# A search for the sample's best 256 keys: from 32 partitions to 128, with TensorE adding the parts

## The reference

```python
def _dsa_attend(q, qi, wi, kv, kidx, q_pos):
    n_sel = min(DSA_TOPK_MAX, lk // 4)
    ...
        idx_s = jnp.einsum('bthd,bsd->bths', qib, kidx) * (IDX_DIM ** -0.5)
        score = jnp.einsum('bth,bths->bts', wib * (IDX_HEADS ** -0.5), jax.nn.relu(idx_s))
        score = jnp.where(causal[None], score.astype(jnp.float32), NEG)
        top_s, top_i = lax.top_k(score, n_sel)
        ok = top_s > 0.5 * NEG
        kvs = kv[b_ix, top_i]
        ...
        p = _masked_softmax(s, ok[:, :, None, None, :])
        o = jnp.einsum('btghn,btngd->btghd', p.astype(kvs.dtype), kvs[:, :, :, 1])
```

## Time and profile before

| | us |
|---|---|
| median of 3 runs | 2259.28 |
| lowest and highest of them | 2257.66, 2259.74 |
| the profiled execution's own time | 2261.38 |
| its span in the profile | 2259.6 |
| PE busy, share of the span | 1815.2, 80% |
| DVE busy | 1120.3, 50% |
| ACT busy | 497.0, 22% |
| POOL busy | 264.0, 12% |

### The profile page before, as it was taken

The page is one execution under the profiler, slowest core; times in us unless marked ns, Lnnn a source line. Parts: engine busy times, 40 slices in busy tenths (PEclk is TensorE's granted clock), DMA queues, the critical chain, the costliest instruction groups (busy, mean ns, idle before and its releaser), DMA issues. The chain is left out here.

```text
span 2259.6 us, 27405 instructions
## 1 busy us (share of the span) xinstructions
PE 1815.2 (80%) x10205; PEld 1046.9 (46%) x10205; DVE 1120.3 (50%) x2591; ACT 497.0 (22%) x1087; POOL 264.0 (12%) x358
## 2 busy tenths in 40 slices
PE   7589999976999988967999878777866775377776
PEld 2367666633445434426666545454533332134332
DVE  0211682275777631223136999726646898021223
ACT  0300001054655400021111000024424331010111
POOL 0011020001544200000010000011122220000000
PEclk9799999987999987988999999888978897598888
DMA  6431351042000076601111101000020000999851
GB/s 250 172 132 61 109 204 63 1 155 76 1 1 1 1 249 162 171 22 63 38 61 36 39 20 39 20 0 1 1 75 1 1 1 7 266 212 227 218 160 36
DMA packets 85872, 189.31 MB, mean 84 GB/s; under 512 B 11531, under 2 KB 48493, under 8 KB 77226
## 3 DMA queue, kind: packets, MB, share of 16 engines
q1 hardware_dynamic: 57996, 120.13, 17.6%
q0 software_dynamic: 10464, 46.45, 5.9%
q10 hardware_dynamic: 17280, 20.98, 3.9%
HBM read 172.57 MB, written 19.12 MB: 85 GB/s over the span
## 5 line engine op out<-in xcount | busy, mean ns | idle before, releaser
L714 PE MATMUL banks<-hT,w_in 128*128 128x352 f32 x1632 | 492.1, 463 | 39.8 <-DVE qdT L782 18.8
L714 PEld LDWEIGHTS banks<-hT,w_in 128*128 128x128 f32 x1632 | 309.8, 191 | 219.3 <-DVE qdT L782 21.1
L2212 PE MATMUL banks<-w_out,mix 128*128 128x512 f32 (+1 forms) x576 | 269.9, 627 | 4.9 <-DVEq L2722 2.5
L710 PE MATMUL banks<-w_in,hT 128*128 128x264 f32 (+5 forms) x1008 | 221.9, 376 | 15.3 <-DMA w_in<-in_w_in 15.3
L710 PEld LDWEIGHTS banks<-w_in,hT 128*128 128x128 f32 (+1 forms) x1008 | 174.3, 188 | 51.5 <-DMA w_in<-in_w_in 15.6
L2212 PEld LDWEIGHTS banks<-w_out,mix 128*128 128x128 f32 (+1 forms) x576 | 107.4, 190 | 153.1 <-issue 146.4
L2228 DVE TENSOR_TENSOR y<-banks,gate_rows 128x512 f32<-128x512 f32 x32 | 22.1, 691 | 232.7 <-PE banks L2212 232.7
L1297 POOL TENSOR_SCALAR nsa_p<-nsa_p,nsa_sum,gates 128x640 f32<-128x640 f32 (+7 forms) x128 | 100.5, 796 | 226.2 <-DVE nsa_sum L1242 226.2
L824 ACT ACTIVATE mix<-banks 128x352 f32<-128x352 f32 x48 | 21.9, 464 | 412.4 <-PE banks L714 382.7
L1134 ACT ACTIVATE nsa_p<-nsa_p,nsa_negmax 128x640 f32<-128x640 f32 (+7 forms) x128 | 92.6, 725 | 29.0 <-DVE nsa_negmax L1123 28.5
L1123 DVE CUSTOM_DVE_ANT_0 nsa_p<-banks,wide_masks 128x640 f32<-128x640 f32 (+7 forms) x128 | 84.0, 703 | 22.7 <-PE banks L1109 22.7
(11 more groups left out here) (492 smaller groups left out, 2431.9 us busy)
## 6 DMA issues: line engine op xcount, KB each, us to landing
w_in<-in_w_in SPq DMA_DIRECT2D x24, 1056.0 KB, 5.0
ada_w<-in_ada SPq DMA_DIRECT2D x24, 1024.0 KB, 4.8
ds_ring<-in_diff_pairs SPq DMA_DIRECT2D x88, 256.0 KB, 5.5
ns_ring<-in_sel_pairs SPq DMA_DIRECT2D x88, 128.0 KB, 2.9
ds_ring<-in_dsa_pairs SPq DMA_DIRECT2D x88, 128.0 KB, 3.1
ds_ring<-in_diff_pairs ACTq DMA_DIRECT2D x40, 256.0 KB, 7.2
w_out<-in_l_w_out SPq DMA_DIRECT2D x4, 2048.0 KB, 20.6
ns_ring<-in_sel_pairs ACTq DMA_DIRECT2D x40, 128.0 KB, 4.2
```

The lines of the kernel that those rows point to most:

```text
L710: last = pe.matmul(bank[0:rows, 0:n], k.hT[:, a, r0:r0 + rows], w[:, j % slots, a, 0:n], start=(a == 0), stop=(a == KT - 1))
L714: last = pe.matmul(bank[:, 0:cn], w[:, j % slots, a, m * P:(m + 1) * P], k.hT[:, a, c0:c0 + cn], start=(a == 0), stop=(a == KT - 1))
L2212: last = pe.matmul(k.bank[u % 2][0:n, :], k.mix[:, a, r0:r0 + n], self.w[:, a, h * 512:(h + 1) * 512], start=a == 0, stop=a == KT - 1)
```

## The change

The class `SampleSearch` replaces `top_mask` for the sample. Each query's scores are laid on four partitions of 512 (the 32 scores of the new keys lie beside the fourth part; the other three have a very small number there), so one count covers 128 partitions x 544. Its sum, `search_seen`, is one column of 128 partial counts. PE multiplies it with a 128x128 matrix that has a 1 where two partitions belong to the same query, and every partition then finds the query's total in bank 7 (`total`). VectorE waits for it (`totalled`) and goes on with three small operations in place of four. The scan and the last passes stay as they were, on 32 partitions.

```diff
-def attend_pairs(k, name, units, base, blocks=None, between=None):
+def attend_pairs(k, name, units, base, blocks=None, between=None, search=None):
...
-        out_bank = lambda u: k.bank[6 + units[u]["tile"] % 2]
+        out_banks = 2 if search is None else 1
+        out_bank = lambda u: k.bank[6 + units[u]["tile"] % out_banks]
...
-                    if begin and i >= 2:
-                        pe.wait_ge(A.finished, i - 1)
+                    if begin and i >= out_banks:
+                        pe.wait_ge(A.finished, i - out_banks + 1)
...
                     turn(u, x)
+                    if search:
+                        search.add_parts(pe)
                     if behind:
                         values(*behind)
...
+                if search:
+                    for _ in range(3):
+                        next(between)
...
-                    while ended and e - ended[0][0] >= 2:
+                    while ended and e - ended[0][0] >= 2 and not search:
                         finish(ended.pop(0)[1])
...
                     copy(u, x)
+                    while ended and search:
+                        finish(ended.pop(0)[1])
...
+class SampleSearch:
...
+    def add_parts(self, pe):
+
+        if self.n < self.counts:
+            self.n += 1
+            pe.wait_ge(self.counted, self.n)
+            pe.matmul(self.total, self.same[:, :], self.seen[:, :], start=True, stop=True).then_inc(self.totalled, 1)
+
+    def count(self, dve, v, threshold, op):
+        dve.tensor_scalar(self.ge, v, threshold, None, op, ALU.add, accum_out=self.seen[:, :]).then_inc(self.counted, 1)
+
+    def steps(self, dve):
...
+        self.count(dve, v[:, :], 0.0, ALU.is_ge)
+        yield
+        dve.wait_ge(self.totalled, 1)
+        link(dve.tensor_scalar(found[:, :], self.total, float(TOPK), -1.0, ALU.is_lt, ALU.mult))
+        for n, bit in enumerate(range(30, -1, -1)):
+            link(dve.tensor_scalar(tried[:, :], found[:, :], 1 << bit, None, ALU.bitwise_xor))
+            self.count(dve, upper[:, :] if bit >= 16 else v[:, :], tried[:, :].bitcast(F32), ALU.is_ge)
+            yield
+            dve.wait_ge(self.totalled, n + 2)
+            link(dve.tensor_scalar(step[:, :], self.total, float(TOPK), float(1 << bit), ALU.is_ge, ALU.mult))
+            link(dve.tensor_tensor(found[:, :], found[:, :], step[:, :], ALU.bitwise_xor))
```

More of the change, by code:

```diff
@@ L1727, in dsa_prompt @@
             sample_index(k, ws)
-            choice = top_mask(k, k.nc.vector, ws, "sample_top", [(k.sample_score[:, :], k.sample_sel[:, :])], TOPK, NS,
-                              scratch=k.qiT[0:NS, :, :].rearrange("p a n -> p (a n)"))
-            attend_pairs(k, "dsa", units, 4, None, chain(keep_dsa_sample(k, k.nc.vector), choice))
+            search = SampleSearch(k, ws, k.qiT[0:NS, :, :].rearrange("p a n -> p (a n)"))
+            attend_pairs(k, "dsa", units, 4, None, chain(keep_dsa_sample(k, k.nc.vector), search.steps(k.nc.vector)), search)
@@ new lines, with __init__ @@
+class SampleSearch:
+    PART = PAST // 4
+    def __init__(self, k, st, scratch):
+        self.k, self.scratch = k, scratch
+        self.v = k.sb(st, "search_scores", [P, self.PART + NS])
+        self.upper = k.sb(st, "search_upper", [P, self.PART + NS], BF16)
+        self.upto = k.sb(st, "search_upto", [P, PAST + NS])
+        self.ge = self.upto[:, :].bitcast(BF16)[:, 0:self.PART + NS]
+        self.found, self.tried, self.step = (k.sb(st, f"search_{x}", [P, 1], I32) for x in ("found", "tried", "step"))
+        self.seen = k.sb(st, "search_seen", [P, 1])
+        self.of_query = k.sb(st, "search_of_query", [P, NS])
+        self.same = k.sb(st, "search_same_query", [P, P])
+        self.need = k.sb(st, "search_need", [NS, 1])
+        self.counted = k.sem(st, "search_counted")
+        self.totalled = k.sem(st, "search_totalled")
+        self.total = k.bank[7][:, 0:1]
+        self.counts, self.n = 33, 0
+    def add_parts(self, pe):
[6 more added lines that the diff above has]
+    def steps(self, dve):
+        k, v, upper, found, tried, step = self.k, self.v, self.upper, self.found, self.tried, self.step
+        link = lambda ins: k.dve_order.link(dve, ins)
+        score, m = k.sample_score, k.sample_sel
+        link(dve.tensor_reduce(self.of_query[:, :], k.const("ident").rearrange("p (x n) -> p n x", n=NS), X, ALU.add))
+        dve.tensor_copy(self.same[:, :].rearrange("p (x n) -> p x n", n=NS), self.of_query[:, :].unsqueeze(1).to_broadcast([P, P // NS, NS]))
+        dve.memset(v[0:3 * NS, self.PART:], TAKEN)
+        for j in range(4):
+            last = dve.tensor_copy(v[NS * j:NS * (j + 1), 0:self.PART], score[:, self.PART * j:self.PART * (j + 1)])
+        link(dve.tensor_copy(v[3 * NS:, self.PART:], score[:, PAST:PAST + NS]))
+        link(dve.tensor_copy(upper[:, :], v[:, :].bitcast(BF16)[:, 1:2 * (self.PART + NS):2]))
+        self.count(dve, v[:, :], 0.0, ALU.is_ge)
[9 more added lines that the diff above has]
+            link(dve.tensor_tensor(found[:, :], found[:, :], step[:, :], ALU.bitwise_xor))
+        kth = found[:, :].bitcast(F32)
+        self.count(dve, v[:, :], kth, ALU.is_gt)
+        yield
+        dve.wait_ge(self.totalled, self.counts)
+        kth, equal = kth[0:NS], self.scratch[:, 0:PAST + NS]
+        link(dve.tensor_scalar(self.need[:, :], self.total[0:NS], -1.0, float(TOPK), ALU.mult, ALU.add))
+        link(dve.tensor_scalar(equal, score[:, :], kth, None, ALU.is_equal))
+        yield
+        link(dve.tensor_tensor_scan(self.upto[0:NS, :], k.const("ones", NS)[:, 0:1].to_broadcast([NS, PAST + NS]), equal, 0.0, ALU.mult, ALU.add))
+        yield
+        link(dve.scalar_tensor_tensor(equal, self.upto[0:NS, :], self.need[:, :], equal, ALU.is_gt, ALU.mult))
+        link(dve.scalar_tensor_tensor(m[:, :], score[:, :], kth, equal, ALU.is_lt, ALU.add))
+        link(dve.tensor_scalar(m[:, :], m[:, :], NEG, None, ALU.mult))
```

## The result

The changed kernel takes 2204.3 us (median of 4 runs, 2199.88 to 2206.78) against 2259.51 us before (median of 4 runs, 2257.66 to 2272.97), or 55.2 us less. The ratio on record is 0.9729, 95% interval 0.9707 to 0.9752; the two medians themselves divide to 0.9756. The forecast was 2209 us.

The account below looks back on a forecast made before the run. The prediction took VectorE, mostly its search counts, to bound the stage. The loop's 142.0 us plus 7 of allowances and a 4.8 us later start made 153.8 against 203.8, 50 us less: 2209 us, range 2196 to 2228.

Parts of the forecast that it names:

- Counts and small operations: In the search loop, shorter counts and three small operations a step in place of four take 55 us off VectorE.
- The later start: At the stage's opening, copied queries and search setup, 6.3 us together, delay the first maxima by about 4.8 us.
- An add: On PE, each of 33 products that total the counts costs 0.3 us, with bounds of 0.14 and 0.54.
- PE becomes the bound: In steps without scores, PE runs through at 2.35 us a step and VectorE's 2.05 are hidden.
- lockstep rival: Counts end after PE reaches the add, 3.5 us a step; if in half of 36 steps, 2229 us; 18%.
- One bank (part 4): One output bank replaces two: a tile's first products wait for the previous multiplication out; PE loses 1.2 us in the last tile.
- The loop: First transposes to last multiplication: 15.4 us for tiles 0 and 1, 97.7 for 2 to 6, 28.9 for 7; 142.0.
- allowances: In the loop, 4 us for partly half clock and 3 us for the way between engines, making 149.
- half-clock rival: PE keeps the half clock in this stage and the kernel is 34 us slower, 2293 us; 4%.
- The sum: For the stage, 149 us, or 153.8 with the delayed opening, against 203.8: 50 us less.

Follow-up runs that it names:

- short counts: Kernel before with every count over 544 of 2080 columns on its 32 partitions, no adds or new layout: stage 156.99 us, median 2207.59 us.
- early start: Changed kernel with query copies and same-query matrix made in the stage ahead, search setup behind the first maxima: stage 145.42 us, median 2204.19 us.

## Why the prediction was right

The time was right, and the mechanism in its main part: VectorE bounded the stage by its counts, the counts were cut to a third, and the stage got shorter by what VectorE lost. Step by step:

- **Counts and small operations, 55 us off VectorE.** Right: 0.78 us a count, and of the 61.8 us that VectorE's work in the loop fell by, 5.9 only moved ahead of the loop, which leaves 55.9. The short counts alone take 54.6 us off the stage. The Trainium skill (VectorE: DVE Perf Modes, "The perf-mode tier table") would have a bf16 count at about half the time of an fp32 one; the groups show 779 ns for both, so the trace disagrees again.
- **The later start, 4.8 us.** Measured 4.9, but not by its terms: 6.3 us of work less a wait of 1.75 make 4.55. The work took 5.9 us (1706.21 to 1712.15), and only 1.06 of the wait could hide it, since VectorE still idles 0.69 us ahead of the work. That the start lay on the path, the early start shows by giving 4.4 of it back.
- **An add, 0.3 us.** Too much. It is 0.31 us from an add to the products only where PE has waited; where PE runs through it is 0.21, and the step grows by 0.11 to 0.12 (2.15 against 2.03 or 2.04), a little under the lower bound of 0.14. The second add of a doubled pair costs 0.22.
- **"PE becomes the bound" with VectorE's 2.05 us hidden.** The step that failed, though it did not cost the forecast. It holds in about half of the steps, those in which PE runs through, 2.15 us without scores in place of the 2.35 laid out; in most of the others PE waits for VectorE, which is not hidden there, and over the loop either one's microsecond counts for 0.6. The lockstep rival fails by its own sign: PE waits 4.9 us for counts, under the 10 that it named, and VectorE never for a total.
- **One bank (part 4).** It was priced as a loss of 1.2 us in the last tile; PE waits 1.04 there. But the earlier place of the multiplication, which comes with it, is worth 7.3 us in the kernel before, 5.7 with short counts and 7.9 in the changed one. The prediction laid the changed lists out with that place and so had it in its 142.0; it did not see it as a gain, and the 15.0 us of VectorE's waits before, on a line of their own, 12.8 of them such waits, were not read.
- **The loop, 142.0 laid out and 149 with allowances.** Measured 137.0: 14.4 for tiles 0 and 1 (15.4), 94.3 for tiles 2 to 6 (97.7), 28.4 for tile 7 (28.9). The layout was 5 us long, 3.4 of them in tiles 2 to 6: PE's work was 85.1 us there, with the shorter adds in it, where 87.3 were laid out, and it idled 9.2 against 10.4. The 7 us of allowances were not needed: the granted clock was 0.84 only in the first 14.4 us, behind a stretch in which PE had worked 4.1 of 12.8 us, then 1.00 for 94.3 with PE busy 85.1, and 0.95 at the end, so the half-clock rival was far off. The Trainium skill (TensorE: Matmul & The Clock Gate, Part 1) says that activity lifts the clock; the trace agrees.
- **The sum.** The stage shrank by 61.8 us where 50 were forecast, but the two profiles' spans differ by 54.7 only: the profile that the sum was made against had a next stage near the short end of its spread, 343.4 in 341.9 to 352.1. An error of 12 us in the stage and one of 7 us about its neighbours, which were held fixed, went in opposite directions. With the neighbours as before, 61.8 us less would have made a median of 2197.5 us, inside the stated range of 2196 to 2228 but outside the 2200 to 2220 that had most of the chance. Beside the changed kernel's second set of runs the medians differ by 59.5 us (2265.74 and 2206.21). So the hit at 2209 is better than the working, and in part luck.

The stage's 61.8 us divide by the experiments, in the order of the kernels run, into 54.6 for the counts, 5.7 for the early place, and 1.5 for the rest: 4.9 lost at the start and 6.4 won in the loop, which is rid of that work, net of the adds, whose doubling cost 4.3. In the other order the early place has 7.3 and the counts 53.0. What the adds cost as they stand was not measured by itself.

## What to carry to other kernels

Ahead of a list of costs, read for the engine that bounds a stage not only what it does but every place where it idles: an engine that is nearly full and still waits 15 us (12.8 of them avoidable here) may have a second gain in the order of its list, and a change that moves an instruction there takes it along. Where a cut brings two engines to equal work, each bounds some of the steps: price a microsecond on either by a fraction (here 0.6), found by doubling one operation and halving the other, and look step by step at which one answers. Work that a change has to add goes where its engine idles anyway, in the stage ahead or behind the first work of its own, which gave 4.4 us here; and an operation that fills 32 partitions costs its columns, so it is worth a layout change to the last of a chain, not only to its counts.

## What the runs showed of the hardware

- A tensor_scalar with a running sum and a threshold for each partition costs by its columns: 0.50, 0.78 and 2.37 us for 272, 544 and 2080 columns, so 1.04 ns a column and 0.21 us beside, in fp32 as in bf16 (779 ns for both). On 32 partitions 544 columns take 0.77 us (short counts), so a quarter of the partitions saves nothing to speak of. I had expected 0.43 us for 272 columns.
- The scan has two ns a column: 1.29 us for 128x544 and 4.47 for 32x2080, (4.47 - 1.29)/1536 = 2.07 ns. A pass of two tensors and a scalar has one: 0.79 and 2.36 us.
- An fp32 product of 128x128 weights with one moving column lengthens a step in which PE runs through by 0.11 to 0.12 us, and a second one by 0.22 (2.03, 2.15 and 2.37 us from transposes to transposes).
- What lies ahead of the stage takes 1699.5 to 1713.0 us in the twelve profiles, though the 40.0 to 41.6 us directly ahead of it hardly vary, and the stage behind 341.9 to 352.1, with the same instructions in it; there the transfers' engines are busy 0.71 to 0.74 of the time. The stage itself, whose share of transfers is 0.00 to 0.01, repeats to 0.01 us.
